# A hybrid DeltaNet / S5 encoder trunk on one core: the S5 recurrence in chunks of four tokens, its matrices formed during the MLP of layer 0

## What is computed

```python
u = hn @ w_in
ug = u.reshape(bsz, seq, 128, 16)                      # 128 groups of 16 channels
lam_bar = exp(lam * step)                              # (128, 64) complex
b_bar = b * ((lam_bar - 1) / lam)[..., None]           # (128, 64, 16) complex
bu = einsum('bsgc,gpc->bsgp', ug, b_bar)
x_t = lam_bar * x_{t-1} + bu_t                         # over 256 tokens, 128 * 64 complex states
y = einsum('bsgp,gcp->bsgc', x, c).real + d_skip * u
vg = gelu(y) @ w_out
return vg[..., :D_MODEL] * sigmoid(vg[..., D_MODEL:])
```

## Time and profile before

| | us |
|---|---|
| median of 3 runs | 3583.05 |
| lowest, highest | 3581.61, 3595.81 |
| the profiled execution | 3587.62 |
| its span, first to last instruction | 3586.0 |
| TensorE busy | 3333.3 (93%) |
| vector engine busy | 2435.3 (68%) |
| ScalarE busy | 1799.9 (50%) |
| GpSimd busy | 746.8 (21%) |
| mean granted TensorE clock (1 is full speed) | 0.967 |

### The profile page before, as it was taken

The page is one execution under the profiler, slowest core; times in us unless marked ns, Lnnn a source line. Parts: engine busy times, 40 slices in busy tenths (PEclk is TensorE's granted clock), DMA queues, the critical chain, the costliest instruction groups (busy, mean ns, idle before and its releaser), DMA issues.

```text
span 3586.0 us, 60991 instructions
## 1 busy us (share of the span) xinstructions
PE 3333.3 (93%) x19058; PEld 2812.4 (78%) x19058; DVE 2435.3 (68%) x4397; ACT 1799.9 (50%) x3770; POOL 746.8 (21%) x969
## 2 busy tenths in 40 slices
PE   6899999999989999999999877787999999999986
PEld 5788888889878888888888654444888888888875
DVE  4889888877745676557655469888557755775544
ACT  3555555565644554445444355554445544454433
POOL 0888888800000000000000025553000000000000
PEclk7999999999999999999999988888999999999998
DMA  4444444444456666666664542232666666666633
GB/s 131 118 123 124 122 127 119 130 118 120 114 150 183 189 184 182 187 176 187 176 186 127 142 131 76 62 90 61 174 173 178 187 181 188 185 192 174 178 110 102
DMA packets 1003986, 525.29 MB, mean 146 GB/s; under 512 B 34448, under 2 KB 998032, under 8 KB 1003392
## 3 DMA queue, kind: packets, MB, share of 16 engines
q1 hardware_dynamic: 998080, 507.06, 51.2%
q0 software_dynamic: 5824, 17.21, 1.5%
HBM read 511.61 MB, written 12.62 MB: 146 GB/s over the span
## 4 chain that ended last, share of the span: by engine, by line
PE 69%; DVE 15%; ACT 6%; issue 5%; DMA 3%; SPq 1%; DVEq 0%; POOL 0%; ACTq 0%; POOLq 0%
PE bank L260 39%; PE bank L261 20%; DVE w_lo L248 4%; PE bank L563 4%; DMA raw<-in_ple_w_gate_dram 2%; DVE y L1467 1%; ACT rot L833 1%; PE bank L303 1%; ACT L833 1%; ACT w_hi L242 1%; DVE x L1684 1%; ACT T L833 1%; DVE y L1464 1%; DVE rb L1730 1%; DVE conv_f L1461 1%
## 5 line engine op out<-in xcount | busy, mean ns | idle before, releaser
L260 PE MATMUL bank<-act,w_hi 128*128 128x512 f32 x4352 | 1610.7, 411 | 25.3 <-DVE w_lo L248 19.7
L248 DVE TENSOR_TENSOR w_lo<-raw,w_hi 128x512 fp32r<-128x512 f32 x1856 | 1240.9, 720 | 215.0 <-ACT w_hi L242 200.8
L261 PE MATMUL bank<-act,w_lo 128*128 128x256 f32 x4352 | 1226.6, 282 | 0.0
L260 PE MATMUL bank<-mid,w_hi 128*128 128x512 f32 x3072 | 1102.8, 403 | 23.0 <-DVE mid L1644 12.6
L242 ACT ACTIVATE w_hi<-raw 128x512 fp32r<-128x512 f32 x1856 | 1041.3, 619 | 156.3 <-PE bank L261 70.7
L260 PEld LDWEIGHTS bank<-act,w_hi 128*128 128x128 f32 x4352 | 828.6, 190 | 244.8 <-DVE w_lo L248 30.8
L261 PE MATMUL bank<-mid,w_lo 128*128 128x256 f32 x3072 | 863.9, 281 | 0.0
L261 PEld LDWEIGHTS bank<-act,w_lo 128*128 128x128 f32 x4352 | 832.1, 191 | 5.0 <-issue 3.6
L260 PEld LDWEIGHTS bank<-mid,w_hi 128*128 128x128 f32 x3072 | 582.6, 190 | 164.8 <-DVE mid L1644 13.9
L261 PEld LDWEIGHTS bank<-mid,w_lo 128*128 128x128 f32 x3072 | 585.3, 191 | 1.6
L270 ACT ACTIVATE tiles<-bank 128x256 f32<-128x256 f32 x384 | 145.7, 380 | 666.0 <-PE bank L261 665.6
(11 more groups left out here) (264 smaller groups left out, 3276.0 us busy)
## 6 DMA issues: line engine op xcount, KB each, us to landing
raw<-in_mlp_w_up_dram SPq DMA_DIRECT2D x128, 1024.0 KB, 6.3
raw<-in_mlp_w_down_dram SPq DMA_DIRECT2D x128, 1024.0 KB, 5.9
raw<-in_gdn_w_in_dram SPq DMA_DIRECT2D x96, 1024.0 KB, 5.8
raw<-in_gdn_w_out_dram SPq DMA_DIRECT2D x32, 1024.0 KB, 6.1
raw<-in_ple_w_gate_dram SPq DMA_DIRECT2D x32, 1024.0 KB, 5.9
raw<-in_s_w_out_dram SPq DMA_DIRECT2D x32, 1024.0 KB, 6.2
raw<-in_s_w_in_dram SPq DMA_DIRECT2D x16, 1024.0 KB, 6.1
turns_scratch<-tiles POOLq DMA_DIRECT2D x64, 128.0 KB, 2.0
```

The source lines that it names most:

```text
L248: eng.tensor_tensor(w_lo[par][:, c], raw[slot][:, c], w_hi[par][:, c].bitcast(F32), ALU.subtract).then_inc(S("lo_ready"), 1)
L260: eng.matmul(a[:, :], w_hi[par][:, w], rhs[:, k0 + kt, :], start=(k0 + kt == 0), stop=False)
L261: mm = eng.matmul(a[:, 0:NT], w_lo[par][:, w], rhs[:, k0 + kt, 0:NT], start=False, stop=(k0 + kt == kend - 1))
```

## The change

S5 runs in chunks of four tokens. Within a chunk the output comes from a Toeplitz kernel of the last four inputs, between chunks from a state that is kept once per chunk: the scan has 64 steps in place of 256. The matrices for this are formed from the parameters in 32 units of four groups, one unit in each of the 32 rounds of layer 0's MLP (`unit_of`): powers 0 to 3 of lam_bar times B (`b_pow`), powers 1 to 4 times C (`c_pow`), the kernel as their product, and the rotation per chunk (the angle times four, over 64 chunks). GpSimd computes (`s5_unit`), TensorE transposes C after the first chunk of a round (`turn_c`) and, after the fourth, B's powers, and makes the kernel (`turn_b_and_kernel`); ScalarE copies out of PSUM, makes the sines and issues four stores a unit; SP loads the parameters (`s5_parameters`). The DeltaNet heads hold no S5 work any more.

In the S5 stage GpSimd loads these matrices, eight DMAs a tile (`load_b`, `load_r`, `load_c`). TensorE's 16 contraction rows per group are widened to 64 by bringing the four tokens of a chunk side by side: SP stores `u` to DRAM and loads it back in four pieces (`fold_u`), and likewise the GELU's output `z` (`unfold_z`), since the output has four tokens stacked in partitions. D is on the kernel's diagonal, and GELU has two steps on the vector engine and two on ScalarE.

Elsewhere: semaphores of the DeltaNet heads that counted one event each are merged into four shared ones with the same order; the transposes of `p` in ple0 move behind its first chunk and the load of `p` behind the last unit; s5out's first chunk waits for `mid` by quarters.

```diff
@@ sync @@
+            def s5_parameters(v):
+                if not isinstance(v, int) or v:
+                    sp.wait_ge(S("spread"), v)
+                for ri, nm in enumerate(("re", "im")):
+                    sp.dma_start(b_in[:, ri, :, :], one_of(t[f"s5_b_{nm}"][0].rearrange(
+                        "(c r g) p e -> c (g p) r e", g=2, r=2), v)).then_inc(S("bc_in"), 16)
+                    sp.dma_start(c_in[0:64, ri, :], one_of(t[f"s5_c_{nm}"][0].rearrange(
+                        "(c g) e p -> c (g e) p", g=4), v)).then_inc(S("bc_in"), 16)
+                sp.dma_start(d_in[0:64, 0:1], one_of(t["s5_d"][0].rearrange("(c p o) -> c p o", p=64, o=1), v),
+                             allow_slow_non_contiguous=True).then_inc(S("bc_in"), 16)
+            def fold_u(ct, j):
+                sp.wait_ge(S("u_ready"), ct + 1)
+                sp.dma_start(one_of(u_dram, ct), u[:, j % 2, :, :].rearrange("p t c -> p (t c)")).then_inc(S("u_saved"), 16)
+                if not isinstance(ct, int) or ct >= 2:
+                    sp.wait_ge(S("y_done"), ct - 1)
+                sp.wait_ge(S("u_saved"), ct * 16 + 16)
+                src = one_of(u_dram, ct).rearrange("(a g) (t c) -> t g a c", g=32, t=4)
+                for back in range(4):
+                    sp.dma_start(uf[32 * back:32 * back + 32, j % 2, :, :], src[3 - back]).then_inc(S(f"u_in{j % 2}"), 16)
+            def unfold_z(ct, j):
+                sp.wait_ge(S("z_ready"), ct + 1)
+                sp.dma_start(one_of(z_dram, ct), z5[:, j % 2, :]).then_inc(S("z_saved"), 16)
+                if not isinstance(ct, int) or ct >= 2:
+                    sp.wait_ge(S("s5_lo"), ct)
+                sp.wait_ge(S("z_saved"), ct * 16 + 16)
+                src = one_of(z_dram, ct).rearrange("(t g) (a c) -> a g t c", g=32, a=4)
+                for a in range(4):
+                    sp.dma_start(zf[32 * a:32 * a + 32, j % 2, :, :], src[a]).then_inc(S(f"z_in{j % 2}"), 16)
@@ tensor @@
+            def turn_c(v):
+                pe.wait_ge(S("c_spread"), v + 1)
+                if not isinstance(v, int) or v:
+                    pe.wait_ge(S("c_copied"), v)
+                for e in range(2):
+                    mm = pe.transpose(A[:, e * P:(e + 1) * P], c_blk[:, e, :, :].rearrange("p g q -> p (g q)"), ident)
+                mm.then_inc(S("c_turned"), 1)
+            def turn_b_and_kernel(v):
+                pe.wait_ge(S("B_ready"), v + 1)
+                if not isinstance(v, int) or v:
+                    pe.wait_ge(S("b_copied"), v)
+                for a in range(2):
+                    for ri in range(2):
+                        mm = pe.transpose(C[:, (2 * a + ri) * P:(2 * a + ri + 1) * P],
+                                          b_pow[:, a, ri, :, :].rearrange("p t q -> p (t q)"), ident)
+                mm.then_inc(S("b_turned"), 1)
+                pe.wait_ge(S("C_ready"), v + 1)
+                if not isinstance(v, int) or v:
+                    pe.wait_ge(S("k_copied"), v)
+                for a in range(2):
+                    for ri in range(2):
+                        mm = pe.matmul(Dk[32 * a:32 * a + 32, 0:P], b_pow[:, a, ri, 0, :], c_pow[:, a, ri, 0:P],
+                                       start=(ri == 0), stop=(ri == 1))
+                mm.then_inc(S("k_done"), 1)
...
+            def state_inputs(ct, i, j):
+                pe.wait_ge(S(f"u_in{j % 2}"), i * 128 + 64 * (j // 2 + 1))
+                pe.wait_ge(S(f"b_in{j % 2}"), i * 32 + 16 * (j // 2 + 1))
+                if ahead(i, j, -2):
+                    pe.wait_ge(S("rotated_in"), ct - 1)
+                for a in range(4):
+                    for ri in range(2):
+                        mm = pe.matmul((A, B)[j % 2][:, (2 * a + ri) * 64:(2 * a + ri + 1) * 64], m_b[:, j % 2, a, ri, :],
+                                       uf[:, j % 2, a, :], start=True, stop=True)
+                mm.then_inc(S("v_done"), 1)
...
+            def s5_in_tile(i, j):
+                n0, t0 = plan["s5in"][0:2]
+                ct = i * 4 + j
+                state_inputs(ct, i, j)
+                for q in range(QUARTERS):
+                    if ahead(i, j, 2):
+                        multiply(pe, ct + (n0 + 2), q, j % 2, j % 2, act, tile_free=ct + (t0 + 1) if q == 0 else None)
+                    if q == 0 and ahead(i, j, -1):
+                        outputs(ct - 1, *back_one(i, j))
...
+                        if name in unit_of and j == 0:
+                            turn_c(i + unit_of[name])
+                        if name in unit_of and j == 3:
+                            turn_b_and_kernel(i + unit_of[name])
@@ gpsimd @@
-            for r4 in range(4):
-                turns(0, r4)
-            with gp.Fori(1, KT) as ct:
-                for r4 in range(4):
-                    turns(ct, r4)
...
+            def s5_unit(v):
...
+                if some:
+                    gp.wait_ge(S("k_done"), v)
...
+                TT(q3[0], b1[0], w3[0], ALU.mult)
+                st_(TT(q3[1], b1[1], w3[1], ALU.mult))
+                TT(b_pow[:, :, 0, 1:4, :], q3[0], q3[1], ALU.subtract).then_inc(S("spread"), 1)
+                gp.wait_ge(S("spread"), v + 1)
+                TT(q3[0], b1[0], w3[1], ALU.mult)
+                st_(TT(q3[1], b1[1], w3[0], ALU.mult))
+                TT(b_pow[:, :, 1, 1:4, :], q3[0], q3[1], ALU.add).then_inc(S("B_ready"), 1)
...
+                if some:
+                    kernel_diagonal(v - 1)
...
+                gp.wait_ge(S("c_copied"), v + 1)
...
+                TT(q4[0], c1[0], w4[0], ALU.mult)
+                st_(TT(q4[1], c1[1], w4[1], ALU.mult))
+                st_(TT(cp[0], q4[0], q4[1], ALU.add))
+                TT(q4[0], c1[1], w4[0], ALU.mult)
+                st_(TT(q4[1], c1[0], w4[1], ALU.mult))
+                TT(cp[1], q4[0], q4[1], ALU.subtract).then_inc(S("C_ready"), 1)
...
+            s5_unit(0)
+            with gp.Fori(1, UNITS) as v:
+                s5_unit(v)
...
+            def load_b(ct, i, j):
+                gp.dma_start(m_b[:, j % 2, :, :, :].rearrange("p (h a) r q -> p h (a r q)", h=2),
+                             b_dram[idx(ct * 2, 2)].rearrange("h p x -> p h x")).then_inc(S(f"b_in{j % 2}"), 16)
+            def load_r(ct, j):
+                for h in range(2):
+                    gp.dma_start(m_r[:, j % 2, :, 2 * h:2 * h + 2, :].rearrange("p s a n -> p s (a n)"),
+                                 one_of(r_dram, ct * 2 + h)).then_inc(S(f"r_in{j % 2}"), 16)
+            def load_c(ct, j):
+                gp.dma_start(m_c[:, j % 2, :, :, :].rearrange("p (h a) r q -> p h (a r q)", h=2),
+                             c_dram[idx(ct * 2, 2)].rearrange("h p x q -> p h (x q)")).then_inc(S(f"c_in{j % 2}"), 16)
+                rows_ = k_dram[idx(ct * P, P)].rearrange("(a g) k -> g a k", g=32)
+                for back in range(4):
+                    gp.dma_start(m_t[32 * back:32 * back + 32, j % 2, :, :],
+                                 rows_[:, :, 32 * back:32 * back + P]).then_inc(S(f"c_in{j % 2}"), 16)
...
+                gp.wait_ge(S("scanned"), ct + 1)
+                gp.tensor_tensor(x_sin[:, :, :, :], st[:, :, :, :], m_r[:, a, 1, :, :].unsqueeze(2).to_broadcast([P, 4, 2, 64]),
+                                 ALU.mult).then_inc(S("st_read"), 1)
+                if ahead(i, j, -1) and ahead(i, j, 1):
+                    load_r(ct + 1, j + 1)
+                if ahead(i, j, 2):
+                    load_b(ct + 2, i, j)
+                gp.wait_ge(S("st_read"), ct + 1)
+                gp.wait_ge(S("x_turned_by_cos"), ct + 1)
+                if ahead(i, j, -1):
+                    gp.wait_ge(S("y_done"), ct)
+                gp.tensor_tensor(x[:, a, 0, :, :], x_cos[:, :, 0, :], x_sin[:, :, 1, :], ALU.subtract)
+                gp.tensor_tensor(x[:, a, 1, :, :], x_cos[:, :, 1, :], x_sin[:, :, 0, :], ALU.add).then_inc(S("x_ready"), 1)
+                if ahead(i, j, 1):
+                    load_c(ct + 1, j + 1)
```

727 lines of the change are left out of this document (402 added, 325 removed).

## The result

The changed kernel takes 3486.22 us (median of 4 runs, 3480.82 to 3491.89), the kernel before beside it 3585.14 us (4 runs, 3581.61 to 3595.81): ratio 0.9721, 95% interval 0.9702 to 0.974. That is 99 us less, where the forecast had 129. The profiled execution took 3491.89 us, with 3490.2 from its first to its last instruction (its span; before 3586.0). The spans differ by 95.8 us, and this table divides them among the stages. A stage runs from its own first weight load on SyncE's queue to the next stage's; the S5 stage ends with TensorE's first product of the output projection.

What follows compares the result with a forecast made beforehand. GpSimd's turns slow the heads, TensorE bounds layer 0's MLP, the vector engine sets S5. Heads -42, MLP +62, gate stage +2, S5 -151 make -129; 3587.6 - 129 - 4.6 gives 3454, say 3455 us; range 3400 to 3530.

Steps and rivals of the forecast that it cites:

- Heads, -42: DeltaNet heads: without GpSimd's turns ten heads gain 4.0 us each, the first some 2 more; -42 us, bounds -30 to -46.
- the fifth rival: DeltaNet heads: they don't gain, because their 4 us had another cause than GpSimd; 3497 us, chance 0.03.
- MLP, +62: Layer 0's MLP: TensorE has no idle time, so 32 units at 1.95 us add 62 us; bounds 45 and 110.
- the vector stretch: Layer 0's MLP: GpSimd stretches vector work 1.34 times, 443.7 to 595 us, still below 710; cost 0, up to 52 us.
- The second rival: Layer 0's MLP: GpSimd takes time there as it took head time, 7% or 52 us; 3507 us, chance 0.13.
- exclusion at its worst: Layer 0's MLP: each of 512 splits waits out a 0.73 us GpSimd operation, 374 us; sum some 46 us higher.
- GpSimd's chain: Layer 0's MLP: the chained part of a unit takes 13 to 18 us and fits into a round of 24.5.
- the fourth rival: Layer 0's MLP: the unit is longer than the round, TensorE waits for C; 3727 us at 32 us, chance 0.05.
- S5, -151: S5 stage: SP's own order sets 13.1 us a tile, stage 220 us against 371; -151 us, bounds -185 and -100.
- the third rival: S5 stage: TensorE's waits lower its clock, loads land in 5 us, 16 us a tile; 3499 us, chance 0.17.
- The first rival: S5 stage: saves don't queue behind weights, the vector engine sets 11 us a tile; 3423 us, chance 0.14.
- The short runs: S5 loads of u and z: 128 runs of 256 B each, charged nothing; if landings doubled, sum 37 us higher.

Runs made afterwards that it cites:

- before_light_turns: The kernel before with two of the ten GpSimd instructions of a pair's turn left, so the turns are wrong; 3540.41 us against 3583.92.
- m_small: The changed kernel with GpSimd's two 512 KB matrix loads cut to 8 KB each from the S5 stage's fifth tile on; 3452.65 us.
- floor: The changed kernel with four folded-u buffers, S5 weight loads on ScalarE's queue, and GpSimd's two large loads cut to 8 KB from the fifth tile; 3443.79 us.
- fold_first: The changed kernel with SyncE issuing the save and reads of u ahead of the S5 tile's weight load; 3467.14 us.

## Why the prediction was right and where not

The total was in the range (3400 to 3530), and part of its nearness to the forecast is luck. Against the profiled execution the sum was 33 us too low (3490.2 for 3586.0 - 129): S5 and its projection brought 46 us more than forecast, and heads and MLP 17 us less.

**Heads, -42: right** (-46.9). Mechanism and price are both shown by before_light_turns (-40.5); the fifth rival is false.

**MLP, +62: the size nearly, the make-up not** (+50.2). Two errors cancelled, which is luck. The records of a unit are 34 to 45 us, not 62: twelve of them with two seams took 1.2 us, where 0.11 us each and 0.1 a seam gave 1.5. And the vector stretch, priced at 0 because its busy sum stayed below TensorE's, costs 16 us on top of TensorE's and would cost 32 or more alone. The stretch itself came as in the heads (914 over 687 ns, 1.33). The step that failed is the comparison of sums: 591 us of vector work in 789 don't bound the stage, yet single splits land after TensorE wants them. The second rival had this and put it at 52 us. By the Trainium skill (SBUF — State Buffer, Who interferes with whom) exclusion at its worst had been 46 us on top; the trace agrees that the two engines meet, and 16 us is what it cost.

**GpSimd's chain: right.** It ends ahead of the round, and the fourth rival is false.

**S5, -151: the term that failed** (-110). Its sum read "2.0 + 2.5 + 2.0 + 0.5 + 6.1 = 13.1 us a tile". The order on SyncE's queue was right, and so were 6.1 and 2 us for the saves, as long as GpSimd's large loads are away: m_small has 6.5 and 2.3. Left out were GpSimd's 1.5 MB a tile, which I had counted as DMA issues and not as bytes. The terms of the sum, beside the means of SyncE's timeline from the save of u of the 5th tile to that of the 16th (rounded one by one):

| | predicted | changed kernel | m_small |
|---|---|---|---|
| save of u to its reads | 6.1 | 8.1 | 6.7 |
| issuing the four reads | 2.0 | 1.8 | 1.9 |
| from there to the save of z | none | 0.9 | 0.7 |
| save of z to its reads | 2.5 | 3.3 | 2.3 |
| issuing the four reads | 2.0 | 1.8 | 1.9 |
| from there to the next save of u | 0.5 | 1.2 | 1.2 |
| tile | 13.1 | 17.2 | 14.5 |

The two saves took 2.8 us more than their terms, and m_small takes 2.5 of that away. Another 1.7 us were left out as well, and 1.3 of them stay in m_small: SyncE waits until z and u themselves are made (changed kernel, 2118 to 2320 us). The issues took 0.4 us less, which makes the 4.1.

```profile
SPq L475 <- DVE z L1923: 9.1, 6, 2.1
SPq L464 <- DVE u L1939: 8.8, 7, 5.0
```

The 13.0 us tile of floor is no proof of the sum, since its saves of u take 2.4 us. On GpSimd the turn by the sine took 2.19 us where the sum had 1.3. What came is near the third rival, "the S5 tile stays slow" at 16 us and 3499 us: from the first to the last state inputs (2120.66 to 2365.20) a tile is 16.3 us. Of its two causes the landings beside other traffic are shown. How much the lower clock adds was not separated; in these runs it was higher where the waits were shorter (0.78 in the changed kernel, 0.88 in floor). I gave this rival 0.17, too little beside 0.48 for a sum that had no traffic in it. The first rival, no queueing behind weights, is false: fold_first moved the save in front of them and it fell from 8.1 to 2.6 us.

The short runs were charged nothing, and nothing speaks against it: reads of u landed in a median of 1.8 us against 2.0 for the old load. But those beside GpSimd's loads were slower. The last of the four came 3.1 us after the first issue in the tile at 2206.64 and 6.1 us in the tile at 2191.45, and both have the same runs. The Trainium skill (DMA: Bandwidth & Descriptors, Specifications) has 512 B as the least for line rate; no run here changed the length of the runs, so that their price is not shown.
